# A decoder layer on one core: the first branch projection pair fed in another order, its token blocks split earlier, and two mixer details moved

## The reference

```python
h = rms_norm(x, norm_w)
proj = jnp.einsum('btd,de->bte', h, w_in) + b_in
(a_q, a_k, a_v, a_z, m_q, m_k, m_v, m_i, m_f, m_o, m_z, g_attn, g_mlstm) = jnp.split(proj, SPLIT_IDX, axis=-1)
attn = sliding_window_sink_attention(a_q, a_k, a_v, attn_sinks)          # first mixer, 16 heads
branch_a = jnp.einsum('bte,ed->btd', attn * jax.nn.silu(a_z), w_branch_attn)
...
h_tilde = mlstm_chunkwise(mq, mk, m_v, m_i, m_f)                         # second mixer, 8 heads, chunks
h_m = jax.nn.sigmoid(m_o) * head_rms_norm(h_tilde, mlstm_norm_w) * jax.nn.silu(m_z)
branch_m = jnp.einsum('bte,ed->btd', h_m, w_branch_mlstm)
merged = jax.nn.sigmoid(g_attn) * branch_a + jax.nn.sigmoid(g_mlstm) * branch_m
return rms_norm(x + jnp.einsum('btd,de->bte', merged, w_out), final_norm_w)
```

## Time and profile before

| | |
|---|---|
| device time, median of 3 runs | 1072.31 us (1072.2 to 1073.39) |
| profiled execution, device time | 1072.99 us |
| its span in the trace | 1071.3 us |
| granted clock of TensorE, mean | 0.998 |
| TensorE busy | 1053.1 us (98%) |
| VectorE, ScalarE, GpSimd busy | 774.6, 539.8, 687.8 us |

### The profile page before, as it was taken

One profiled execution on the slowest core, in us unless ns is written; L12 is line 12 of the kernel. 1 busy time (PEld: TensorE's weight loads), 2 busy tenths in 40 slices (PEclk: granted clock), 3 DMA queues, 4 the chain that ended last, 5 costly groups with the idle time before them and its releaser, 6 DMA issues.

```text
span 1071.3 us, 18681 instructions
## 1 busy us (share of the span) xinstructions
PE 1053.1 (98%) x6343; PEld 853.0 (80%) x6343; DVE 774.6 (72%) x1186; ACT 539.8 (50%) x1286; POOL 687.8 (64%) x469
## 2 busy tenths in 40 slices
PE   7999999999999999999999999999999899999997
PEld 6887887877877888888878888888777788788886
DVE  5964785776866967776776686769588647766897
ACT  7544755746646643554445454545466345113543
POOL 3577555556555569668966797569859984635441
PEclk9999999999999999999999999999999999999999
DMA  6225132132151232224313433232329439676424
GB/s 221 71 93 90 41 119 80 41 119 74 44 158 49 80 118 80 83 56 137 119 51 92 126 92 94 88 117 89 102 94 376 137 118 330 205 275 260 166 99 137
DMA packets 122078, 131.79 MB, mean 123 GB/s; under 512 B 7884, under 2 KB 97288, under 8 KB 120472
## 3 DMA queue, kind: packets, MB, share of 16 engines
q1 hardware_dynamic: 107048, 84.42, 25.7%
q10 hardware_dynamic: 14960, 46.47, 12.7%
HBM read 96.16 MB, written 34.70 MB: 122 GB/s over the span
## 4 chain that ended last, share of the span: by engine, by line
PE 88%; POOL 3%; DVE 2%; DMA 2%; ACT 1%; DVEq 1%; POOLq 1%; issue 0%; ACTq 0%; SPq 0%
PE ps L1104 66%; PE ps L1407 5%; PE ps L1011 4%; PE ps L1221 3%; POOL ring_lo L836 2%; PE ps L1202 2%; PE ps L1276 2%; PE ps L1348 1%; POOL t L831 1%; PE ps L1330 1%; PE ps L1345 1%; DVE u_m L2704 1%; PE ps L1342 1%; PE ps L1296 1%; PE ps L1363 1%; DMA ev<-gm_scratch 1%
## 5 line engine op out<-in xcount | busy, mean ns | idle before, releaser
L836 POOL TENSOR_TENSOR ring_lo<-w,ring_hi 128x512 fp32r<-128x512 f32 x144 | 213.3, 1503 | 86.8 <-ACT ring_hi L1539 86.8
L836 POOL TENSOR_TENSOR ring_lo<-t,ring_hi 128x512 fp32r<-128x512 f32 x108 | 152.2, 1414 | 141.3 <-ACT ring_hi L1539 141.3
L1104 PE MATMUL ps<-s_hi,ring_hi 128*128 128x512 f32 x576 | 228.7, 397 | 1.8 <-issue 1.8
L1104 PE MATMUL ps<-s_lo,ring_hi 128*128 128x512 f32 x576 | 225.1, 391 | 0.0
L1104 PE MATMUL ps<-s_hi,ring_lo 128*128 128x512 f32 x576 | 225.0, 391 | 0.0
L1104 PE MATMUL ps<-h_hi,ring_hi 128*128 128x512 f32 x432 | 170.7, 395 | 2.6 <-POOL ring_lo L836 1.4
L1104 PE MATMUL ps<-h_lo,ring_hi 128*128 128x512 f32 x432 | 169.0, 391 | 0.0
L1104 PE MATMUL ps<-h_hi,ring_lo 128*128 128x512 f32 x432 | 168.6, 390 | 0.0
L1539 ACT ACTIVATE ring_hi<-w 128x512 fp32r<-128x512 f32 x144 | 86.7, 623 | 110.4 <-PE ps L1104 93.7
L1104 PEld LDWEIGHTS ps<-s_hi,ring_hi 128*128 128x128 f32 x576 | 108.2, 188 | 26.0 <-issue 5.1
L1104 PEld LDWEIGHTS ps<-s_hi,ring_lo 128*128 128x128 f32 x576 | 108.2, 188 | 22.4
(11 more groups left out here) (317 smaller groups left out, 2072.0 us busy)
## 6 DMA issues: line engine op xcount, KB each, us to landing
w<-in_w_in SPq DMA_DIRECT2D x128, 256.0 KB, 2.9
xs<-in_x SPq DMA_DIRECT2D x8, 512.0 KB, 8.2
ga_scratch<-ev ACTq DMA_DIRECT2D x4, 1024.0 KB, 4.1
u_scratch<-silu_z ACTq DMA_DIRECT2D x8, 512.0 KB, 3.2
c_rows<-c_scratch ACTq DMA_DIRECT2D x8, 512.0 KB, 6.7
ev<-u_scratch SPq DMA_DIRECT2D x8, 512.0 KB, 4.6
u_sums_scratch<-ev ACTq DMA_DIRECT2D x4, 1024.0 KB, 5.0
gm_scratch<-ev ACTq DMA_DIRECT2D x4, 1024.0 KB, 5.1
```

The source lines that it names most:

```text
L836: return nc.gpsimd.tensor_tensor(flat(lo[:]), flat(raw_or_sum[:]), flat(hi[:]).bitcast(F32), ALU.subtract)
L1104: mm = nc.tensor.matmul(ps[:, bank, columns], w[:, k, :], h[:, k, columns], start=(m == 0), stop=(m == PRODUCT - 1))
```

## The change

- **Second mixer.** The sum block 5 (`s1`) is now split there too: ScalarE copies its high part into `us_hi`, VectorE subtracts, and both parts are stored and later loaded (two transfers of 1024 KB instead of one). The store of each step is cut in two stages (three transfers, then two). `branch_sums` comes one chunk earlier, `gated_z` and ScalarE's `store_gm` move by some instructions, and the wait for the store moves from ScalarE to VectorE.
- **First branch pair (32).** TensorE's twelve matmuls of each product go by term: four high x high, then four with the low weights, then four with the low tokens, and it waits for each part where it is first used. The low parts of weight blocks 2 and 7 go from GpSimd to VectorE (`weights_low`). VectorE and ScalarE no longer split block 5.
- **Second branch pair (33).** GpSimd interleaves the sums and the low parts; the load of `w21` stands behind that of `w12`. `normalised_h` of the last step is done in pair 33 rather than 32, `turn_h` and `gated_h` follow three products later, and ScalarE asks for the gate rows after product 5 of pair 32 rather than after product 7.
- **Ends of mixer steps 0 to 2.** `turn_h` stands at position `count * PAIR - 4` rather than `- 14`. VectorE's order there is unchanged.
- **Output weights.** A `drain` goes, and the subtraction of `f_s2` moves from tile 1 to tile 2.

```diff
@@ gpsimd
+            def first_branch_pair(i):
+                first_sum(i)
+                second_sum(i)
+                third_sum()
+                low_1(i)
+                low_6(i)
+                fourth_sum(i)
+                low_4(i)
+                low_5(i)
+                low_3(i)
+
+            def second_branch_pair(i):
+                first_sum(i)
+                low_1(i)
+                second_sum(i)
+                low_6(i)
+                third_sum()
+                low_2(i)
+                fourth_sum(i)
+                low_7(i)
...
@@ tensor
-                    more(count * PAIR - 14)
+                    more(count * PAIR - 4)
                     turn_h(p)
...
+                def in_parts(n, ring_slot, w_low):
+                    hi, lo = BLOCKS[n]
+                    if n < 5:
+                        pe.wait_ge(u_hi, n + 1)
+                    else:
+                        pe.wait_ge(u_in[n], 32)
+                    part(product_bank(n, None), ring_slot[0], hi, first=True)
+                    pe.wait_ge(w_low, i + 1)
+                    part(product_bank(n, None), ring_slot[1], hi)
+                    if n < 5:
+                        pe.wait_ge(u_split, n + 1)
+                    return part(product_bank(n, None), ring_slot[0], lo, last=True)
...
                 elif a == 1:
-                    pairs(WPAIRS + 1, 0, 3 * PRODUCT)
+                    pairs(WPAIRS + 1, 0, 6 * PRODUCT)
                     turn_h(PAIRS - 1)
@@ scalar
-                    if q == 3 and not last:
+                    if q == (3 if a else 5) and not last:
@@ vector
+            def weights_low(ring_slot, raw_or_sum, high_made, ready):
+                dve.wait_ge(high_made, WPAIRS + 1)
+                V.tensor_tensor(ring_slot[1][:], raw_or_sum[:], ring_slot[0][:].bitcast(F32), ALU.subtract).then_inc(ready, 1)
...
                     V.tensor_tensor(f_s3[:], f_o11[:], f_o21[:], ALU.subtract).then_inc(wo_sum, 1)
-                    dve.drain()
+                if n == 2:
                     V.tensor_tensor(f_s2[:], f_s1[:], f_o11[:], ALU.subtract)
-                if n == 2:
```

More of the change, by code:

```diff
@@ L875, in _, with lows_of_pair, weights_of_pair @@
             sums(0)
[L877 to L893, removed]
+            def lows_of_pair(i):
+                low_2(i)
[3 more added lines that the diff above has]
+                low_5(i)
+            def weights_of_pair(i, hook=None):
+                lows_of_pair(i)
+                sums(i + 1, hook)
+            def first_branch_pair(i):
[5 more added lines that the diff above has]
+                fourth_sum(i)
+                low_4(i)
+                low_5(i)
+                low_3(i)
+            def second_branch_pair(i):
+                first_sum(i)
+                low_1(i)
+                second_sum(i)
+                low_6(i)
+                third_sum()
+                low_2(i)
+                fourth_sum(i)
+                low_7(i)
+                low_3(i)
+                low_4(i)
+                low_5(i)
             def last_branch_sums():
@@ L1367, in _, with first_branch_pair, part @@
             ended(pe, PAIRS, mlstm_step)
+            def first_branch_pair(i):
+                def part(bank, weights, tokens, first=False, last=False):
+                    for k in range(KH):
+                        mm = nc.tensor.matmul(ps[:, bank, :], weights[:, k, :], tokens[:, k, :], start=first and k == 0,
+                                              stop=last and k == KH - 1)
+                    return mm
+                def in_parts(n, ring_slot, w_low):
[10 more added lines that the diff above has]
+                    return part(product_bank(n, None), ring_slot[0], lo, last=True)
+                pe.wait_ge(w1_hi, i + 1)
+                pe.wait_ge(c21_out, i)
+                in_parts(0, ring0, w1_ready).then_inc(p1_done, 1)
+                pe.wait_ge(w6_hi, i + 1)
+                pe.wait_ge(c22_out, i)
+                in_parts(1, ring1, w6_ready).then_inc(p6_done, 1)
+                pe.wait_ge(w2_hi, i + 1)
+                pe.wait_ge(c12_out, i)
+                in_parts(2, ring2, w2_ready).then_inc(p2_done, 1)
+                pe.wait_ge(w7_hi, i + 1)
+                pe.wait_ge(c_out, i)
+                in_parts(3, ring3, w7_ready).then_inc(p7_done, 1)
+                pe.wait_ge(w4_hi, i + 1)
+                pe.wait_ge(a_copied, i + 1)
+                in_parts(4, ring0, w4_ready).then_inc(p4_done, 1)
+                pe.wait_ge(w5_hi, i + 1)
+                pe.wait_ge(b_out, i + 1)
+                in_parts(5, ring1, w5_ready).then_inc(p5_done, 1)
+                pe.wait_ge(w3_hi, i + 1)
+                pe.wait_ge(c11_out, i + 1)
+                in_parts(6, ring4, w3_ready).then_inc(p3_done, 1)
@@ L2513, in after_gm @@
                 def after_gm(q):
+                    if q == 3:
+                        dve.wait_ge(us_out, US_ALL * (p + 1))
                     after(q, i0 + 3, (R_GM + 2 * p, R_GM + 2 * p + 1), ev_part)
                     if last:
-                        for n in {2: (0,), 5: (1,), 6: (2, 3)}.get(q, ()):
-                            block_low(n)
+                        if q == 2:
+                            block_low(0)
+                        if q == 4:
+                            block_low(1)
+                        if q == 6:
+                            weights_low(ring2, w21, w2_hi, w2_ready)
+                            block_low(2)
+                            weights_low(ring3, w12, w7_hi, w7_ready)
+                            block_low(3)
                 def after_next(q):
```

165 lines of the change are left out of this document (105 added, 60 removed).

## The result

The changed kernel takes 1081.88 us (median of 6 runs, 1079.75 to 1082.64) beside 1072.26 us (6 runs, 1072.05 to 1076.07). The ratio is 1.0077, its 95% interval 1.0064 to 1.0091: some 8 us slower, where I had forecast 0.4 us faster. The two medians lie 9.6 us apart.

A forecast was written before the change was run, and what follows sets the result against it. TensorE, busy for 1053.1 of 1071.3 us, was taken as the bound, so only its waits matter. 2.1 (step ends) - 1.3 (pair 33) - 1.2 (output weights) = -0.4 us: median 1071.9, range 1068.7 to 1073.9.

The forecast's parts named there:

- the rest of the mixer's edits I cost at nothing: Second mixer: extra copy, subtraction, issues and earlier branch_sums cost nothing; without cover, some 2 us a step.
- a new wait inside the mixer's chunks: Second mixer: listed among the signs that would show the forecast wrong, given no size.
- Ends of the steps: Mixer steps 0 to 2: later turn_h makes product 6's additions late, 0.7 us three times, 2.1 us lost.
- rival 2: Mixer steps 0 to 2: the ends of the steps cost nothing, 2.1 us better, 1069.8 us; chance 0.13.
- Pair 32: First branch pair: no wait before products 2 and 7, product 4 0.5 us late; 0.7 us of waits with restart.
- the sum on the transfers: Pair 32: 1024 KB more loading takes 2.7 us; block 6 lands at 830.8, hidden by 1.6 us.
- Rival 4: Pairs 32 and 33: queues take turns, w12 lands near 835, product 6 1 us later, 1072.9 us; chance 0.08.
- Pair 33: Second branch pair: product 6 earlier, products 4 and 5 wait 1.5 and 0.7 us; pair 34 starts 1.3 us earlier.
- rival 3: Pair 33: gate rows land late, high part 4 and product 4 come 3.5 us later, 1075.4 us; chance 0.11.
- rival 1: Pair 33: products 4 and 5 do not wait, 2.2 us better, 1069.7 us; chance 0.16.
- Output weights: Output weights, tile 3: f_s2 moves behind VectorE's PSUM read, so TensorE's wait goes; 1.2 us gained.

The follow-up runs named there:

- e1: Changed kernel with both gated_z of a mixer step put back behind the additions of their chunk: 1074.15 us, ratio 1.0006.
- e4: Kernel before the change with only gated_z moved ahead of the additions of its chunk: 1074.16 us, ratio 1.0003.
- e13: Changed kernel with ScalarE's four split steps spread over later chunks and VectorE's second low part in chunk 5 instead of 4: 1073.86 us, ratio 1.0002.
- e3: Changed kernel with turn_h of steps 0 to 2 back at 14 matmuls ahead of the step's end instead of 4: 1080.71 us, ratio 1.0066.
- e6: Changed kernel with gated_z and turn_h both back in their old places in steps 0 to 2: 1073.89 us, ratio 1.0005.
- e12: Kernel before the change with only the output weights' edit, f_s2 behind tile 1's read: 1071.65 us, ratio 0.9983.
- e8: Changed kernel, gated_z and turn_h back, gate store later; in pair 33 first low part ahead of first sum, turn_h 4 matmuls before the end: 1072.12 us.
- e10: Changed kernel, gated_z back, gate store later, turn_h at 9 (pair 33: 4), pair 33's first low part on VectorE: 1070.58 us, ratio 0.9963.
- e2: Changed kernel with only chunk 7's gated_z put back behind the additions, chunk 6's staying ahead: 1075.03 us, ratio 1.0013.

## Why the prediction was wrong

**The step that failed** is "the rest of the mixer's edits I cost at nothing". The cover that I named, 72% and 50% of busy time and no wait of TensorE in the mixer, is no cover: it says nothing of the order in which an engine comes to the work that TensorE needs. I had written what it would cost without cover, 2 us a step; it was 1.7 in steps 0 and 2 and 4.6 in step 1, where the clock fell, 8.0 in all, and another 0.2 to 0.3 a step in chunk 5. It takes two edits together:

1. ScalarE's split steps were put into the chunk in which VectorE makes what they wait for. ScalarE stands 4.2, 6.6 and 5.2 us; high parts and `mz_part` come late, and VectorE is 2.2 us late at chunk 6. Its idle time of 1.85 us before chunk 7 takes up most of that, but there it meets two GpSimd instructions that it had just missed before. In e1 the addition that product 6 needs ends 2.5 us later than before (483.94, 481.40). Alone this costs next to nothing.
2. `gated_z` ahead of the additions takes 2.0 us of what product 6 has to spare. Alone it costs nothing (e4).

e13 takes the first away, e1 the second, and the 8 us go with either. Both draw on the same cover, which I had never measured: the 3.0 us by which the addition before was ahead of product 6. What is left of it is 1.0 us with the second edit alone (e4; an estimate, since its row joins two additions) and 0.6 with the first alone (e1); with both, the addition ends 4.8 us later than before (486.2, again an estimate from a joined row): 1.4 because VectorE comes late to the chunk, 1.3 for `den`, 2.1 for `gated_z`. That is more than the cover, and the wait is 1.43. The list of what would prove me wrong did name "a new wait inside the mixer's chunks", without a chance or a price; it should have been the slower rival.

**Ends of the steps.** Forecast 0.7 us each; measured 0.51 and 0.16 for the restart. Right in place, releaser and size; rival 2 falls. Going back gained about half of it in e3, where a longer stretch at the lower clock took 1.2 us, and next to nothing in e6, where `turn_h` waited instead.

**Pair 32.** No wait before products 2 and 7, as forecast, and none before product 4. There were two others: 0.36 us for a low part of GpSimd in product 1, and 1.08 us for block 6 (`s_lo`). The second is the sum on the transfers: hidden by 1.6 us, I had said, and it missed by 1.1. Rival 4 had the mechanism, and the landing of `w12` too (19.8 us behind the start of pair 32, where it said 19.5), but too small a price, 1.0; the sharing delays block 6 as well.

**Pair 33.** Product 6 starts 22.6 us after product 6 of pair 32 (24.8 before), not 21.6: block 6, product 1 and product 6 wait 2.8 us between them. The gate rows landed in 3.8 us (rival 3 falls). Products 4 and 5 did not wait (that much of rival 1 came true); but `normalised_h` is late, and `turn_h` waits 1.07 us for it, a wait that I had not looked at. Product 1 waits 1.46 us: its low part stands behind a sum that waits for `w12`. So this stretch gained 0.44 us instead of 1.3.

**Output weights.** Forecast 1.2 us; 0.9 by the starts, in e12 1.0 by the starts and 1.5 in the medians.

## What to carry to other kernels

Before costing moved work at nothing, read the end of the instruction that TensorE next needs from that engine and the start of the matmul that needs it; the difference is the cover, and every edit on that engine and on those that it waits for draws on the same one. Do not place a step in the chunk where its operand is made: an engine that stands in order holds up everything behind it. When two waits pull an instruction to both sides, look for a place between them (14, 4, then 9).

## What the runs showed of the hardware

- **A short operation can pay for a long neighbour.** `den` of 128x2 elements with two operands in SBUF took 0.16 us, or 1.15 to 1.18 when a GpSimd instruction of 128x512 elements (1.30 us) had started 0.12 to 0.16 us before it; where GpSimd's started 0.05 us behind it, it took 0.16. The reciprocal beside it, with one operand, took 0.17 at 482.66 with GpSimd busy. The Trainium skill ("SBUF — State Buffer", Who interferes with whom) says that a VectorE instruction with two SBUF inputs contends with a GpSimd instruction that reads SBUF, that the shared ports are an exclusive lock, and that issue order decides who blocks, not the operation's shape; the trace agrees.
- **The clock's fall is part of a wait's price.** Idle times of 2.66 (after, e3), 1.88 (e8) and 2.60 us (e10) were followed by a stretch at 1.2 GHz; those of 1.83 (e1), 1.80 (e2) and 1.43 us were not. The stretch cost 1.6 us (after, e8), 1.7 (e10) and 2.9 (e3), so the same wait can have two prices.
- **SyncE can stand at issuing.** With several loads of 1024 KB under way, the issue of a weight load took 4.57 us (at 828.97, after), where in pairs 32 and 33 before none took more than 0.84. Such issues are not new: before, one took 8.06 us (at 930.13), in the second branch projection. Nothing was seen to wait for the one at 828.97 alone: the next load, `w12`, was issued at 833.73, and the low part that it waits for ended at 833.71.
